# The projections, norms, heads and rotations of a transformer block's input made one stage

## What is computed

```python
h = rms_norm_2(x, norm1_gain[l]) * (1.0 + sc1) + sh1
z = h @ w_in[l]
(c_q, c_kv, k_pe, q_n, k_c, v_c, k_s, v_s, k_w, v_w,
 g_nsa, g_mla_merge, g_nsa_merge) = jnp.split(z, split_at, axis=-1)
...
q = (rms_norm_2(c_q, q_a_gain) @ w_q_b).reshape(B, S, MLA_HEADS, MLA_QK)
kv = (rms_norm_2(c_kv, kv_a_gain) @ w_kv_b).reshape(B, S, MLA_HEADS, MLA_NOPE + MLA_V)
k_nope, v = kv[..., :MLA_NOPE], kv[..., MLA_NOPE:]
k = jnp.concatenate([k_nope, jnp.broadcast_to(k_pe[:, :, None, :], (B, S, MLA_HEADS, MLA_ROPE))], axis=-1)
q = rms_norm_2(q, q_gain)
k = rms_norm_2(k, k_gain)
...
q = partial_rope(rms_norm_2(q, q_gain), cos_t, sin_t)
ks = partial_rope(rms_norm_2(k_s, ks_gain), cos_t, sin_t)
kw = partial_rope(rms_norm_2(k_w, kw_gain), cos_t, sin_t)
```

## Time and profile before

| | us |
|---|---|
| median of 3 runs | 6181.12 (6163.56 to 6197.46) |
| profiled execution, its own time | 6154.41 |
| its span | 6152.8 |
| TensorE busy in the span | 5069.8 (82%) |
| VectorE busy | 2762.7 (45%) |
| ScalarE busy | 1112.2 (18%) |
| GpSimd busy | 514.8 (8%) |

### The profile page before, as it was taken

The page is one execution under the profiler, slowest core; times in us unless marked ns, Lnnn a source line. Parts: engine busy times, 40 slices in busy tenths (PEclk is TensorE's granted clock), DMA queues, the critical chain, the costliest instruction groups (busy, mean ns, idle before and its releaser), DMA issues. The chain is left out here.

```text
span 6152.8 us, 91837 instructions
## 1 busy us (share of the span) xinstructions
PE 5069.8 (82%) x38874; PEld 3885.4 (63%) x38874; DVE 2762.7 (45%) x3766; ACT 1112.2 (18%) x1605; POOL 514.8 (8%) x396
## 2 busy tenths in 40 slices
PE   9996979997989986667695995774599777699988
PEld 7776879996866663333584884324355456588876
DVE  5665534444356634747444543162333355422222
ACT  3342222223212200001121001101121233101100
POOL 0002322210005600000000000030100000000000
PEclk9998989998999997888888997855597788899999
DMA  3433131112133335141313522422300113222233
GB/s 136 150 132 101 54 114 53 52 52 76 55 121 113 115 128 182 41 164 68 133 50 110 178 103 78 147 77 72 79 4 8 39 34 130 98 73 72 68 133 133
DMA packets 265825, 572.95 MB, mean 93 GB/s; under 512 B 29282, under 2 KB 123921, under 8 KB 264746
## 3 DMA queue, kind: packets, MB, share of 16 engines
q1 hardware_dynamic: 191606, 382.48, 19.1%
q10 hardware_dynamic: 53056, 111.69, 4.8%
q0 software_dynamic: 20816, 73.69, 3.5%
HBM read 388.69 MB, written 179.08 MB: 92 GB/s over the span
## 5 line engine op out<-in xcount | busy, mean ns | idle before, releaser
L464 PE MATMUL gu_ps<-kept_h_hi,gu_w_hi 128*128 128x512 f32 x704 | 275.2, 391 | 40.0 <-DVE gu_w_lo L122 40.0
L464 PE MATMUL gu_ps<-kept_h_lo,gu_w_hi 128*128 128x512 f32 x704 | 275.0, 391 | 0.0
L464 PE MATMUL gu_ps<-kept_h_hi,gu_w_lo 128*128 128x512 f32 x704 | 274.8, 390 | 0.0
L464 PE MATMUL win_ps<-kept_hn_hi,win_w_hi 128*128 128x512 f32 x576 | 226.4, 393 | 48.0 <-DVE win_w_lo L122 48.0
L1735 PE MATMUL front_product<-kept_x_hi,front_w_hi 128*128 128x512 f32 x544 | 222.5, 409 | 10.3 <-DVE kept_x_lo L122 10.1
L464 PE MATMUL win_ps<-kept_hn_lo,win_w_hi 128*128 128x512 f32 x576 | 225.9, 392 | 0.0
L464 PE MATMUL win_ps<-kept_hn_hi,win_w_lo 128*128 128x512 f32 x576 | 225.7, 392 | 0.0
L1735 PE MATMUL front_product<-kept_x_hi,front_w_lo 128*128 128x512 f32 x544 | 215.3, 396 | 0.0
L1735 PE MATMUL front_product<-kept_x_lo,front_w_hi 128*128 128x512 f32 x544 | 215.1, 395 | 0.0
L3138 PE MATMUL lc_ps<-idft,lc_zz 128*128 128x256 f32 x512 | 120.9, 401 | 90.8 <-DVE lc_zz L3016 90.8
L2703 PE MATMUL oproj_product<-kept_h_hi,oproj_w_hi 128*128 128x512 f32 x384 | 158.4, 412 | 25.0 <-DVE kept_h_lo L122 20.1
(11 more groups left out here) (718 smaller groups left out, 12140.7 us busy)
## 6 DMA issues: line engine op xcount, KB each, us to landing
s_decayed<-front_ring SPq DMA_DIRECT2D x96, 256.0 KB, 4.0
...
win_mod_w<-in_ada_w POOLq DMA_DIRECT2D x8, 2048.0 KB, 10.4
...
```

Source lines behind the costliest of these rows:

```text
L464: mm = pe.matmul(ps[:, u, h, :], a, b, start=(k == 0 and n == 0), stop=(k == kt - 1 and n == len(pairs) - 1))
```

## The change

The eight stages become one (projections, tag win). It walks 49 slots (prep_slots). In 41 of them weights stream in as in linear: 35 tiles of depth 8 and 6 of depth 6, for the query product's output is now packed (the 64 plain rows of two heads to a tile, the 32 rotated rows of four heads to a tile), and the last two part tiles of z are one. The other 8 slots are kn (4) and vm (4), of four float32 products of 512 columns each; a tile of the merge gates stands between each two slots of qb, kn and vm. Everything else is hung into the slots:
- TensorE, inside a tile's walk over k (beside): the sum of squares of the slot before at k = 3, the spreading of inverse roots at k = 2 and 6 in nine slots, transposes at k = 5 in three, the modulation's product in slot 12. The sum has 12 or 8 output columns (for c_kv 128), so one sum serves a whole group of heads.
- ScalarE takes all products out of PSUM, squares them, and applies the gains on the way.
- VectorE divides the weights of slot s + 2 first in its turn s, then does the roots, rotations, scalings and modulation pieces (2 tiles to a piece where there were 4) that the tables by slot list.
- The rotation is done before the norm's factor is applied, and its exchange of rows is done by small DMAs within SBUF (swap), not by a product; GpSimd multiplies by the cosine for 8 tiles where it did 22. GpSimd's queue issues all stores and the modulation's loads; SyncE's queue the weights, the tables and the exchanges.
- c_q, c_kv, the heads before their norm and the turned tiles no longer pass through DRAM.
- The rotation tables move from beside win to beside ogate, in its turns 0 to 3 (start = 0), and carry the sine's sign in their frequencies.

```diff
-    start = 8
+    start = 0
...
     linear(nc, "ogate", [kept], 8, lambda n: a["odd_w"][24 + n], 8, gate, unroll=True,
-           beside=lambda st: Modulation(st, a, mod, 0, 16, 8))
+           beside=lambda st: Several(Modulation(st, a, mod, 0, 16, 8), RopeTables(st, a, c, rope)))
...
+def prep_slots():
+
+    order = [("n", j) for j in range(6)] + [("head", 0), ("kc", 0), ("vc", 0), ("vs", 0), ("vw", 0)]
+    order += [("cq", i) for i in range(6)] + [("ckv", i) for i in range(2)]
+    merge = 0
+    for kind, count in (("qb", 6), ("kn", 4), ("vm", 4)):
+        for i in range(count):
+            order += [(kind, i), ("merge", merge)]
+            merge += 1
+    return order + [("merge", merge), ("merge", merge + 1)]
...
+    STREAM = [s for s, (kind, _) in enumerate(SLOTS) if kind not in ("kn", "vm")]
+    turn_of = {s: n for n, s in enumerate(STREAM)}
+    depth = lambda s: {"qb": 6, "kn": 2, "vm": 2}.get(SLOTS[s][0], 8)
...
+    SPREADS = {9: (("n", 0), ("n", 1)), 10: (("n", 2), ("n", 3)), 11: (("n", 4), ("n", 5)),
+               34: (("q", 0), ("q", 1)), 36: (("q", 2), ("q", 3)), 38: (("q", 4), ("q", 5)),
+               42: (("k", 0), ("k", 1)), 44: (("k", 2), ("k", 3)), 46: (("k", 4), ("k", 5))}
+    TURNED = {13: "gates", 14: "vs", 15: "vw"}
+    MOD_TURNS = {0: (0,), 1: (1, 2), 2: (3, 4), 3: (5, 6), 4: (7, 8), 5: (9,), 6: (10,), 8: (11, 12), 9: (13, 14), 10: (15,)}
+    MB, MOD_LO, MOD_N = 2, 16, 32
...
+                def load(s):
+                    n, (kind, i) = turn_of[s], SLOTS[s]
+                    sp.wait_ge(lower_done, n)
+                    src = a["w_q_b"][i] if kind == "qb" else a["w_in2"][W_TILE[kind][i]]
+                    sp.dma_start(raw[:, 0:depth(s), :], src).then_inc(w_in, 16)
...
+                for s in range(NS):
+                    if s + 3 in turn_of:
+                        load(s + 3)
+                    if s < 6:
+                        sp.wait_ge(evac, s + 1)
+                        sp.wait_ge(roped, s)
+                        sp.wait_ge(zeroed, 1)
...
+                    if s == 29:
+                        sp.wait_ge(prod, 30)
+                        sp.dma_start(kn_w, a["w_kn"]).then_inc(kv_w_in, 16)
+                        sp.dma_start(v_w, a["w_v"]).then_inc(kv_w_in, 16)
...
+                def beside(s, k):
+                    if k == 3 and s >= 1 and s - 1 in sums:
+                        sum_squares(s - 1)
+                    if s in SPREADS and k in (2, 6):
+                        spread_out(SPREADS[s][k // 4])
+                    if s in TURNED and k == 5:
+                        turn_tokens(TURNED[s])
+                    if s == 12 and k == 6:
+                        pe.wait_ge(pb_used, user["mod"])
+                        pe.wait_ge(added, 8 * MOD_N // MB)
+                        for n in range(MOD_N):
+                            mm = pe.matmul(pb[:, 0, n:n + 1], acc[:, n, :], one[:, :], start=True, stop=True)
+                        mm.then_inc(pb_done, 1)
...
+                for s, (kind, i) in enumerate(SLOTS):
+                    u = s % 2
+                    if s >= 2:
+                        pe.wait_ge(evac, s - 1)
+                        if SLOTS[s - 2][0] == "cq":
+                            pe.wait_ge(cq_lo_done, SLOTS[s - 2][1] + 1)
+                    if s in turn_of:
+                        n = turn_of[s]
+                        pe.wait_ge(lower_done, n + 1)
+                        if (kind, i) == ("qb", 0):
+                            pe.wait_ge(cq_lo_done, 6)
+                        hi, lo = (cq_hi, cq_lo) if kind == "qb" else (hn.hi, hn.lo)
+                        for k in range(depth(s)):
+                            beside(s, k)
+                            for h in range(2):
+                                half = slice(h * H2, (h + 1) * H2)
+                                pairs = parts((w_hi[:, n % 2, k, :], w_lo[:, n % 2, k, :]), (hi[:, k, half], lo[:, k, half]))
+                                for m, (l, b) in enumerate(pairs):
+                                    mm = pe.matmul(pp[:, u, h, :], l, b, start=(k == 0 and m == 0),
+                                                   stop=(k == depth(s) - 1 and m == 2))
+                        mm.then_inc(prod, 1)
...
+                def turn_rows(n, out, by_cos_, rows_, swaps, tables):
+
+                    dve.wait_ge(tab_in, tables)
+                    dve.wait_ge(swapped, swaps)
+                    dve.tensor_tensor(xs[0:rows_, :], xs[0:rows_, :], cs[0:rows_, 1, :], ALU.mult).then_inc(by_sin, 1)
+                    dve.wait_ge(by_sin, n + 1)
+                    dve.wait_ge(by_cos, n + 1)
+                    dve.tensor_tensor(out, by_cos_, xs[0:rows_, :], ALU.add).then_inc(roped, 1)
+
...
+                def mod_turn(n):
+                    u = n % 2
+                    dve.wait_ge(mod_in[u], 16 * (n // 2 + 1))
+                    ch = Chain(dve, added, 8 * n)
+                    part = acc[:, MB * n:MB * n + MB, :]
+                    ch(dve.tensor_scalar(part, mw[:, u, :, 0, :], silu_c[:, 0:1], None, ALU.mult))
+                    for k in range(1, 8):
+                        ch(dve.scalar_tensor_tensor(part, mw[:, u, :, k, :], silu_c[:, k:k + 1], part, ALU.mult, ALU.add))
...
+                for s, (kind, i) in enumerate(SLOTS):
+                    dve.wait_ge(prod, s + 1)
+                    divide(s + 2)
+                    if kind == "cq":
+                        dve.wait_ge(evac, s + 1)
+                        dve.scalar_tensor_tensor(cq_lo[:, i, :].bitcast(F32R), flat(pp[:, s % 2, :, :]), gains[:, G_CQ + i:G_CQ + i + 1],
+                                                 cq_hi[:, i, :], ALU.mult, ALU.subtract).then_inc(cq_lo_done, 1)
+                    if s == 6:
+                        dve.wait_ge(summed, 6)
+                        take_root(flat(pm)[0:12, :], RMS_EPS, 12)
+                    if 1 <= s <= 6:
+                        turn_rows(s - 1, x[:, s - 1, :], rope_cos[(s - 1) % 2], P, 64 * s, 32)
+                    if s == 7:
+                        invert(ROOT_N, 12, 0)
+                    for n in {8: (0, 1), 9: (2, 3), 10: (4, 5)}.get(s, ()):
+                        scale(("n", n), x[:, n, :], x[:, n, :])
+                    for n in MOD_TURNS.get(s, ()):
+                        mod_turn(n)
+                    if s == 11:
+                        mod_finish()
+                    if s + 1 in TURNED:
...
+                for s, (kind, i) in enumerate(SLOTS):
+                    if kind == "n":
+                        pool.wait_ge(evac, s + 1)
+                        if i >= 2:
+                            pool.wait_ge(roped, i - 1)
+                        by_cosine(rope_cos[i % 2], x[:, i, :], 32)
...
+                        elif kind == "merge":
+                            ring_store(s, rows(outs["merge"], P * i))
...
     norm(nc, "n1", h, 8, hn, None, None, RMS_EPS, c["avg1024"], gains=(mod[:, 48:56], mod[:, 0:8]))
-    linear(nc, "win", [hn], 8, lambda n: a["w_in2"][n], 36, z, unroll=True,
-           beside=lambda st: Several(Modulation(st, a, mod, 16, 48, 4), RopeTables(st, a, c, rope)))
+    kv_raw, merge, vm = dram("kv_raw", 256, T), dram("merge", 2 * D, T), dram("vm", T, 512)
+    qm, km, qn, ksw = dram("qm", D, T), dram("km", D, T), dram("qn", 512, T), dram("ksw", 256, T)
+    vs, vw, gates = dram("vs", T, P), dram("vw", T, P), dram("gates", T, 24)
+    projections(nc, "win", hn, a, c, mod, rope, {"kc": kv_raw[0:P], "vc": kv_raw[P:2 * P], "merge": merge, "vm": vm, "qm": qm,
+                                                 "km": km, "qn": qn, "ksw": ksw, "vs": vs, "vw": vw, "gates": gates})
     hn.free()
-    tile = lambda n, m=1: z[n * P:(n + m) * P]
-    cq, ckv = Kept(nc, "cq", 6, split=True), dram("ckv", 256, T)
-    norm(nc, "ncq", tile(0, 6), 6, cq, None, None, RMS_EPS, c["avg768"], gains=(a["q_a_gain"],))
-    norm(nc, "nckv", tile(6, 2), 2, ckv, None, None, RMS_EPS, c["avg256"], gains=(a["kv_a_gain"],))
-    qb, kn, vm = dram("qb", D, T), dram("kn", 512, T), dram("vm", T, 512)
-    linear(nc, "qb", [cq], 6, w("w_q_b"), 8, qb)
-    cq.free()
-    linear(nc, "kn", [ckv], 2, w("w_kn"), 4, kn, split=False)
-    linear(nc, "vm", [a["w_v"]], 2, lambda n: tiled(ckv)[:, :, ds(n * P, P)], 8, vm, width=H2, split=False)
-    qm, km, qn, ksw = dram("qm", D, T), dram("km", D, T), dram("qn", 512, T), dram("ksw", 256, T)
...
-    head_norms(nc, "heads", loads, a["head_gains"], c, rope, dsts)
-    vs, vw, gates = dram("vs", T, P), dram("vw", T, P), dram("gates", T, 24)
-    to_tokens(nc, "tt", [tile(15), tile(17), z[34 * P + 32:34 * P + 56]], c, [vs, vw, gates], sigmoid=(2,))
     kc, vc = dram("kc", 64, 2 * NCMP), dram("vc", NCMP, 2, 64)
-    compress(nc, "cmp", tile(12), tile(13), a, c, rope[2:4], kc, vc)
+    compress(nc, "cmp", kv_raw[0:P], kv_raw[P:2 * P], a, c, rope[2:4], kc, vc)
```

566 lines of the change are left out of this document (388 added, 178 removed).

## The result

The changed kernel takes 5885.16 us (median of 4 runs, 5862.23 to 5935.33), the kernel before 6172.34 us (4 runs). The ratio is 0.954, with a 95% interval of 0.947 to 0.961. The profiled execution took 5885.1 us beside 6154.4 of before: 269.3 less. TensorE is busy 84% of the span, where it was 82%.

A forecast was written before the change was run, and what follows sets the result against it. TensorE's work and idle time were taken as the bound. The new stage's 556.9 us for 844.8 saves 287.9, ogate adds 14.0: -273.9, giving 5880 from the profiled execution, 5907 from the median; range 5872 to 5960.

The forecast's parts named there:

- slow start: New stage's first microseconds: TensorE runs at the low clock, 2.7 us more.
- waits: Inside the new stage: TensorE waiting on other engines, 5 us taken, bounds 0 and 30.
- what streams is the same 512 columns: Sums of squares with 8 or 12 output columns: priced at 0.43 us an instruction, 43.0 us in all.
- my lower bound: New stage's start, last instruction before to first division: 10.6 us taken, bounds 8.3 and 12.9; division 2.0 more.
- The collision: Turns 1 to 4: GpSimd's cosine product stretches a VectorE instruction from about 1.25 to 2.37 us, 1.1 more a turn.
- My margin of 10.7 less 3: VectorE's weight division may be 10.7 us late before TensorE waits; forecast late by 3 after four turns.
- my second rival: Norm roots in the new stage not hidden: four chains of about 12 us, 48 in all, total 5955; chance 0.07.
- The third rival: Hand-over by slots in the new stage costs 2.5 us in each of 49, 123 in all, total 6030; chance 0.03.
- the slower rival: TensorE loses its high clock in the new stage, falling to 0.50; up to 6438 us; chance 0.03.
- The marks: Signs in the new stage: TensorE busy about 533 us, clock 0.97 or more, VectorE idle near nothing in slots 1 to 4.
- Tail: ogate's end, behind the last tile: fourth rotation table 8.2 us and sine 1.06 before the store.
- the range's lower end: Whole kernel: range 5872 to 5960 us; its low end assumes no waits, better start and ogate, other runs.

## Why the prediction was right

The forecast was 5907 us from the median of three, and 5880 from the profiled execution's own time; that execution's counterpart took 5885.1. By its own steps:

- **TensorE in the stage.** Forecast 538.4 us (530.7, slow start 2.7, waits 5), measured 549.9, from 3335.12 to 3885.05. The product count and its 0.2267 us held within 1.5 us, and kn and vm took their 27.5. The sums of squares were 43.0 at 0.43 an instruction; the instructions cost that, but 21 of the 25 sums have 0.30 more at their borders, a pair that stands together 0.38 and the two full-width ones nothing: +6.6. The spreadings were 16.3, at the pace of the products; one cost 1.33 us where I had 0.91, +7.6 for 18 of them. The modulation's product was 10.1 instead of 9.5, with 2.0 of slow clock behind: +2.6. Transposes -2.0, the slow start -0.8 and waits -4.3 (0.7 instead of 5) go the other way; together 11.2 of the 11.5. The step that failed in size is "what streams is the same 512 columns": it priced each matmul by its columns alone, and narrow ones between full ones cost more. The runs show the extra for the sums (it is gone with one-pass operands); for the spreadings, which were one-pass from the start and have 12 rows, it is read from the rows below and no run takes it away. "Wrong I would be if the sums of squares cost much more than 0.43 an instruction" is the mark that came nearest to being hit: 0.50.

One spreading of slot 10, with the products around it: from 3457.34 to 3459.13 it is 1.79 us, less two steps of 0.227 1.33, where four product steps would be 0.91.

```profile
3457.34 0.39 PE L3490 MATMUL win_product<-kept_hn_hi,win_w_lo 128*128 128x512 f32 x1
3457.66 0.49 PE L3445 MATMUL win_pb<-win_rinv,win_spread 12*128 12x512 f32 x1
...
3458.79 0.50 PE L3490 MATMUL win_product<-kept_hn_hi,win_w_hi 128*128 128x512 f32 x1
3459.13 0.39 PE L3490 MATMUL win_product<-kept_hn_lo,win_w_hi 128*128 128x512 f32 x1
```

- **The start.** Forecast 12.6 with the division, measured 6.8, below my lower bound. I had bounded it by the earlier trace rows, in both of which other transfers go out ahead of the weights or beside them. Issued 0.45 us before GpSimd's 2 MB, the weights arrived 4.0 us after their issue. The run with the weights behind the constants and the 2 MB had 11.43 to the first cast, where it was 4.76.
- **VectorE.** The piece of 256 took the 4.0 us that I had interpolated (0.35 and 3.61 with a gap). The collision did not take 1.1 but 2.5 us in each of turns 2 to 5 (and 2.0 in turns 0 and 1, on other instructions): a turn of 14.85 beside a slot of 12.9. At the head of turn 5, VectorE was late by 7.4 us (3420.16 for a slot that ended at 3412.8), not by 3. The 8.3 us that followed from the Trainium skill's page SBUF — State Buffer, section SBUF: two separate sides (the loser is blocked for the whole instruction), were nearer than my own reading of one row. My margin of 10.7 less 3 would have covered all but 0.1 of 7.8 us more; the run with them shows that it did not. The margin held by about 1 us: the weights of slot 7 were ready at 3424.65 for a slot that began at 3425.7. The forecast was right here with less to spare than it said.
- **The roots.** Hidden, as forecast, the first just so: its spreading waited 0.7 us (3450.88). In the open they cost 53 us: 44 of waits, where my second rival had 48, and 9.5 of slower matmuls, which it had not.
- **The hand-over.** The third rival's 2.5 us a slot were 0: no wait of TensorE at any slot's head.
- **The clock.** 0.99 and not below 0.9: the narrow sums and spreadings never cost it inside dense products. The 64 one-column instructions did, from 4 us into their row (0.50 from 3503 to 3513) to some 4 us behind it. So the slower rival fell.
- **The end.** 5.6 us, forecast 5.9.
- **The marks.** VectorE's idle time in turns 2 to 5 was nothing, as I wrote, but since it was late and not since it was just in time; in slot 1 it still had 5.1 us. TensorE was busy for 549 us, not 533.
- **ogate.** Forecast +14.0, measured +16.3. Tail +9.2 (forecast 9.9), TensorE +2.3 (4.1), and +4.8 at the start, which I had not priced: the first cast came 13.25 us after the first issue and 8.45 before, because the tables' two loads, the positions' broadcast among them, now stand ahead of the first weights in SyncE's queue; with these behind the weights it was 8.4. I had read in the code that it moved, and priced only its VectorE work.

The errors were +11.5 (TensorE), -5.8 (start), -0.3 (end), +2.3 (ogate) and -3 in stages that I had left alone: +4.7 in sum, the 5 us by which 5880 was low. They partly cancelled: that the sum is nearer than its terms is luck. So is part of the range's hit. I had put the median 26.7 us above the profiled execution, as it was before; this time the two are equal, and 5885 lies 13 us above the range's lower end. From median to median the gain is 287 us, where I had 274.

One sentence of the forecast is wrong by its own sum: "the larger half of the gain is the idle time". Its terms give 133 us of idle time and 155 of busy time. Measured it was 143 and 139.
